# A third place for raw weight slabs: the tile of the probabilities, lent to the down projections and to one slab of the third block

## The chip, the cores and the metric

The kernel is one program on one core of a Trainium2 chip. The metric is the device time of a run in microseconds (us). The core's engines are TensorE (PE, matrix products; PEld is its weight load), VectorE (DVE), ScalarE (ACT), GpSimd (POOL) and SyncE (SP), which here only issues transfers. They run side by side and are held together by semaphores.

## The reference: three transformer blocks

The input x is 256 tokens by 1024. Two blocks of one kind run first, then one of another kind; all weights are float32 and each is used once.

```python
for l in range(2):                                   # first block, twice
    a = hybrid_mixer(rms_norm(x, pre_mix_g[l]), ...)
    x = x + rms_norm(a, post_mix_g[l])
    c = memory_cross_attention(rms_norm(x, pre_xattn_g[l]), rms_norm(mem, mem_g[l]), ...)
    x = x + rms_norm(c, post_xattn_g[l])
    hdn = jnp.square(jax.nn.relu(rms_norm(x, pre_mlp_g[l]) @ w_up[l]))
    x = x + rms_norm(hdn @ w_down[l], post_mlp_g[l])
h = rms_norm_2(x, norm_mix_g)                        # third block, once
z = h @ w_in                                         # gate, queries, keys/values, compress_blocks(...)
...
x = x + jnp.square(jax.nn.relu(h @ w_ff1)) @ w_ff2
```

The third block's attention first compresses keys and values with a small gelu network (`cmp_w1`, `cmp_w2`), whose weights are slabs 5 to 8 and 10 of that block.

## The kernel before: one stream of slabs through two raw places

Every weight matrix is cut into slabs of 128 partitions by 2048 float32 (1 MB). Blocks 0 and 1 have 64 slabs each, the third block has 59. A slab takes four steps, each by another engine:

1. SP issues its transfer from HBM into a raw place (`load`, L805; in the third block L837 and L839). There are two places, `raw[:, s % 2]`, so slab s waits until slab s-2 has been read for the last time (semaphore `slab_lo`).
2. ACT rounds it into `w_hi` (`split_hi`, L548). `w_hi` and `w_lo` are rings of three places, so this waits also until TensorE has finished slab s-3 (`slab_used`).
3. DVE subtracts the rounded part from the raw one and writes the rest into `w_lo` (`split_lo`, L558). That frees the raw place.
4. TensorE multiplies with `w_hi` and `w_lo`: 48 matmuls of 256 columns for a slab (for the down projections L2570, L2572, L2574).

Each engine works through a written order, with no scheduler behind it. SP issues slab after slab, in the order of the numbers, and one that waits holds back all behind it. ACT and DVE have `split_hi` and `split_lo` written between their other work, TensorE follows the tables `TE_ORDER` and `TE_ORDER_2`.

In blocks 0 and 1 the up projection is slabs 32 to 47 and the down projection slabs 48 to 63. In the third block they are slabs 27 to 42 and 43 to 58. During the up projection DVE writes each result, scaled and cut at zero, into one of the four places of the tile `probs` (L1656), and ACT squares it from there (`squared_up`, L1005 and L1006; the second counts the semaphore `h_sq`). In blocks 0 and 1 the last of these 16 squarings stands behind the rounding of slab 50 and ahead of that of slab 51. In the third block it stands behind the rounding of slab 45.

After the down projection come the sum of squares over the columns (DVE L1632, L1635; TensorE L2376), the root, the addition to x, and the first slabs of the next block. DVE has `split_lo` of the next block's slabs 0 and 1 ahead of L1632. Besides SP, POOL issues some transfers. During block 1's down projection it loads three tensors for the third block (L890 twice, L892), 1 MB in all as written.

In the third block ACT takes the root of a head's sum of squares in `head_root` (L1212). The third of these stands between the rounding of slab 7 and that of slab 8, with a load of the table for Exp behind it (`load_table`, L959). `head_inverse` on DVE (L1939, L1940) follows the root, and `split_lo` of slab 8 stands behind it. TensorE has the products of slab 7, then a turn (L2694), `head_spread` (L2687), and slab 8.

Of the kernel before, what the change touches and what calls it, by code (L numbers as in the profile page):

```python
# [139 lines left out]

FIRST_VALUES = 4

FIRST_CONSTANTS = 2
# [203 lines left out]
def build(nc, A, out):  # L347
    ctx = ExitStack()
    with ctx:
# [56 lines left out]
        sig = {name: sem(name) for name in PER}  # L406
        raw_loaded = [sem(f"raw_loaded{r}") for r in range(RAW)]
        i_load = {n: sem("i_" + n) for n in ("cst", "x", "mem", "gains", "pos", "relb", "rows", "skew", "toep", "gains_2",
# [126 lines left out]
        def slot(layer, s):  # L535
            return (64 * layer + s) % RING

        def split_hi(act, layer, s):


            loads = s // RAW + 1 + (second(layer) and s >= 3)
            act.wait_ge(raw_loaded[s % RAW], layer * (16 * 32) + 16 * loads)
            if 64 * layer + s >= RING:
                act.wait_ge(sig["slab_used"], value("slab_used", layer, s - RING + 1))
            pieces = split_views_2 if second(layer) else split_views
            views = pieces(s if s < 64 else 0, w_hi[:, slot(layer, s)], raw[:, s % RAW])
            for n, (d, r) in enumerate(views):
                ins = act.activation(d, r, ACT.Copy)  # L548
            ins.then_inc(sig["slab_hi"], 1)

        def split_lo(dve, layer, s):
# [3 lines left out]
            pieces = split_views_2 if second(layer) else split_views  # L555
            for (d, r), (h, _) in zip(pieces(sp, w_lo[:, slot(layer, s)], raw[:, s % RAW]),
                                      pieces(sp, w_hi[:, slot(layer, s)], raw[:, s % RAW])):
                ins = dve.tensor_tensor(d, r, h.bitcast(F32), ALU.subtract)  # L558
# [228 lines left out]
        def _(sp):  # L787
            for name in CREDIT:
# [7 lines left out]
                         A["x"][0].rearrange("(i p) n -> p i n", p=P)).then_inc(i_load["x"], 16)  # L796

            def load(layer, s):

                if (layer, s) in ((0, 0), (0, 1)):  # L800
                    return
                sp.wait_ge(sig["slab_lo"], value("slab_lo", layer, s - RAW + 1))
                src = slab_source(layer, s)
                a, b = src.shape[1], src.shape[2]
                sp.dma_start(raw[:, s % RAW, 0:a * b].rearrange("p (k n) -> p k n", k=a), src)\  # L805
                    .then_inc(raw_loaded[s % RAW], 16)

# [20 lines left out]

            for s in range(59):
                sp.wait_ge(sig["slab_lo"], v2("slab_lo", s - RAW + 1))  # L830
                src = slab_source_2(s)
                n = int(np.prod(src.shape[1:]))
                dst = raw[:, s % RAW, 0:n]
                if s in (3, 4):
                    dst = dst.rearrange("p (k v n) -> p k v n", k=8, v=2)
                    for v in range(2):
                        sp.dma_start(dst[:, :, v], src[:, :, v]).then_inc(raw_loaded[s % RAW], 16)  # L837
                else:
                    sp.dma_start(dst.rearrange("p (k n) -> p k n", k=src.shape[1]), src)\  # L839
                        .then_inc(raw_loaded[s % RAW], 16)  # L840
            for b in range(4):
# [74 lines left out]
        def _(act):  # L916
# [361 lines left out]
            for n in range(2):  # L1278
                act.wait_ge(once["sgw_turned"], n + 1)
                act.activation(sg_w[:, 4 * n:4 * n + 4], bank(f"sgw{n}", DEPTH)[:, :].rearrange(  # L1280
                    "p (g t) -> p g t", g=4), ACT.Copy).then_inc(once["sgw_evac"], 1)
            head_root(2, 8, 1.0, eps_64)
            load_table(ACT.Exp)
            split_hi(act, DEPTH, 8)
            split_hi(act, DEPTH, 9)
# [1653 lines left out]
```

## Time and profile before

| | |
|---|---|
| median of 3 runs | 1248.75 us (1247.89 to 1250.09) |
| the profiled execution | 1255.14 us, of which its span is 1253.3 us |
| PE busy | 1219.3 us, 97% of the span |
| PEld busy | 1188.8 us, 95% |
| DVE busy | 830.8 us, 66% |
| ACT busy | 666.8 us, 53% |
| POOL busy | 47.8 us, 4% |
| read from HBM | 198.50 MB, 159 GB/s over the span |

Busy time of PE is modelled and overlaps from one matmul to the next, so 97% doesn't mean that nothing is left. What is read here are the places where PE waits, and for whom. Times in rows are from the start of the span; the 1.8 us around it belong to the execution as well.

### The profile page before, as it was taken

Reading aid. Unit: us, or ns where it says so; the run is one execution under the profiler, and the core shown is the slowest. Engines: PE = TensorE matmul, PEld = TensorE weight load, DVE = VectorE, ACT = ScalarE, POOL = GpSimd, SP = SyncE. Lnnn points to the kernel's source line nnn. Section 1 sums busy time; section 2 is a strip of 40 time slices with the busy share of each in tenths; the row PEclk is TensorE's granted clock in tenths of the full one; section 3 lists DMA queues with packets and bytes.
Section 4 is the critical chain, followed back from the end, with each engine's and each line's share of the span. In section 5 each row is a group of like instructions: output and inputs, shape, how many; then the busy total and the mean of one; then the engine's idle time right before and its main releaser. Section 6 shows DMA issues by size and latency. Waiting matters only on the chain.

```text
span 1253.3 us, 23254 instructions
## 1 busy us (share of the span) xinstructions
PE 1219.3 (97%) x10089; PEld 1188.8 (95%) x10089; DVE 830.8 (66%) x972; ACT 666.8 (53%) x969; POOL 47.8 (4%) x45
## 2 busy tenths in 40 slices
PE   7999999999999999999999999989999999999998
PEld 6999999999999999999999999989899998999998
DVE  5797467677654678845868666348778875676442
ACT  5586455456544438645645654335486754555432
POOL 2100000000000000000000000100200100000000
PEclk9999999999999999999999999999989999999999
DMA  7735454346656453545434665663451543466552
GB/s 236 211 121 168 136 169 135 122 148 202 203 189 211 126 169 106 167 147 172 154 102 138 215 196 191 210 195 118 142 168 35 166 139 101 135 203 202 198 180 94
DMA packets 194840, 201.06 MB, mean 160 GB/s; under 512 B 5407, under 2 KB 191554, under 8 KB 194739
## 3 DMA queue, kind: packets, MB, share of 16 engines
q1 hardware_dynamic: 193155, 195.50, 48.6%
q0 software_dynamic: 1584, 4.08, 1.3%
q8 instruction: 80, 1.31, 0.5%
q14 instruction: 21, 0.17, 0.0%
HBM read 198.50 MB, written 1.26 MB: 159 GB/s over the span
## 4 chain that ended last, share of the span: by engine, by line
PE 77%; DVE 9%; DMA 5%; ACT 5%; issue 3%; SPq 0%; DVEq 0%; ACTq 0%
PE bank L602 13%; PE bank L603 13%; PE bank L604 13%; PE bank L2572 4%; PE bank L2570 4%; PE bank L2574 4%; DVE w_lo L558 4%; DMA raw<-in_w_down_dram 3%; ACT w_hi L548 3%; PE bank L645 2%; PE bank L653 2%; PE bank L647 2%; PE bank L2480 2%; PE bank L2464 2%; PE bank L701 2%
## 5 line engine op out<-in xcount | busy, mean ns | idle before, releaser
L558 DVE TENSOR_TENSOR w_lo<-raw,w_hi 128x2048 fp32r<-128x2048 f32 (+6 forms) x208 | 419.9, 2029 | 258.7 <-ACT w_hi L548 257.9
L548 ACT ACTIVATE w_hi<-raw 128x2048 fp32r<-128x2048 f32 (+6 forms) x208 | 351.7, 1703 | 336.3 <-PE bank L2574 68.6
L602 PE MATMUL bank<-act_hi,w_hi 128*128 128x256 f32 (+1 forms) x1104 | 307.6, 279 | 1.3 <-DVE w_lo L558 1.3
L604 PE MATMUL bank<-act_hi,w_lo 128*128 128x256 f32 (+1 forms) x1104 | 305.6, 277 | 0.0
L603 PE MATMUL bank<-act_lo,w_hi 128*128 128x256 f32 (+1 forms) x1104 | 305.6, 277 | 0.0
L602 PEld LDWEIGHTS bank<-act_hi,w_hi 128*128 128x128 f32 (+1 forms) x1104 | 206.9, 187 | 3.7 <-issue 3.3
L604 PEld LDWEIGHTS bank<-act_hi,w_lo 128*128 128x128 f32 (+1 forms) x1104 | 206.9, 187 | 0.1
L603 PEld LDWEIGHTS bank<-act_lo,w_hi 128*128 128x128 f32 (+1 forms) x1104 | 206.6, 187 | 0.2
L2570 PE MATMUL bank<-h_hi,w_hi 128*128 128x256 f32 x736 | 203.3, 276 | 0.0
L2574 PE MATMUL bank<-h_hi,w_lo 128*128 128x256 f32 x736 | 203.2, 276 | 0.0
L2572 PE MATMUL bank<-h_lo,w_hi 128*128 128x256 f32 x736 | 203.1, 276 | 0.0
L2572 PEld LDWEIGHTS bank<-h_lo,w_hi 128*128 128x128 f32 x736 | 138.2, 188 | 0.0
L2570 PEld LDWEIGHTS bank<-h_hi,w_hi 128*128 128x128 f32 x736 | 138.1, 188 | 0.0
L2574 PEld LDWEIGHTS bank<-h_hi,w_lo 128*128 128x128 f32 x736 | 138.1, 188 | 0.0
L602 PE MATMUL bank<-w_hi,act_hi 128*128 128x256 f32 (+1 forms) x272 | 78.2, 287 | 0.0
L603 PE MATMUL bank<-w_lo,act_hi 128*128 128x256 f32 (+1 forms) x272 | 76.4, 281 | 0.0
L604 PE MATMUL bank<-w_hi,act_lo 128*128 128x256 f32 (+1 forms) x272 | 76.3, 280 | 0.0
L645 PE MATMUL bank<-act_hi,w_hi 128*128 128x256 f32 x248 | 62.1, 284 | 5.8 <-ACT act_hi L923 5.7
L602 PE MATMUL bank<-o_hi,w_hi 128*128 128x256 f32 (+1 forms) x228 | 64.0, 281 | 0.9 <-issue 0.6
L603 PE MATMUL bank<-o_lo,w_hi 128*128 128x256 f32 (+1 forms) x228 | 63.5, 278 | 0.0
L604 PE MATMUL bank<-o_hi,w_lo 128*128 128x256 f32 (+1 forms) x228 | 63.4, 278 | 0.0
L647 PE MATMUL bank<-act_hi,w_lo 128*128 128x256 f32 x248 | 61.1, 280 | 0.0
(418 smaller groups left out, 2178.3 us busy)
## 6 DMA issues: line engine op xcount, KB each, us to landing
raw<-in_w_up_dram SPq DMA_DIRECT2D x32, 1024.0 KB, 5.4
raw<-in_w_down_dram SPq DMA_DIRECT2D x32, 1024.0 KB, 5.3
raw<-in_w_ff_dram SPq DMA_DIRECT2D x32, 1024.0 KB, 5.3
raw<-in_w_in_dram SPq DMA_DIRECT2D x21, 1024.0 KB, 5.4
raw<-in_w_xk_dram SPq DMA_DIRECT2D x8, 1024.0 KB, 5.3
raw<-in_w_xv_dram SPq DMA_DIRECT2D x8, 1024.0 KB, 5.2
raw<-in_w_mix_out_dram SPq DMA_DIRECT2D x8, 1024.0 KB, 5.2
raw<-in_w_xq_dram SPq DMA_DIRECT2D x8, 1024.0 KB, 5.4
```

What stands on the lines that cost most here:

```text
L548: ins = act.activation(d, r, ACT.Copy)
L558: ins = dve.tensor_tensor(d, r, h.bitcast(F32), ALU.subtract)
L602: pe.matmul(o, stat_hi, mov_hi, start=first, stop=False)
L603: pe.matmul(o, stat_hi, mov_lo, start=False, stop=False)
L604: return pe.matmul(o, stat_lo, mov_hi, start=False, stop=last)
L645: pe.matmul(dst, stat_hi, mov_hi, start=k == 0 and opens, stop=False, skip_group_check=True)
L647: pe.matmul(dst, stat_lo, mov_hi, start=False, stop=False, skip_group_check=True)
L653: ins = pe.matmul(dst, stat_hi, mov_lo, start=False, stop=k == 7, skip_group_check=True)
L701: pe.matmul(dst, wh[:, k, c], src_hi[:, k], start=opens and k == 4 * half and m == 0, stop=False, skip_group_check=True)
L2570: ins = pe.matmul(b[:, T * m:T * m + T], wh[:, k, cs], h_hi[:, 8 * c + k], start=c == 0 and k == 0 and (apart or m == 0), stop=False, skip ...
L2572: pe.matmul(b[:, T * m:T * m + T], wh[:, k, cs], h_lo[:, 8 * c + k], start=False, stop=False, skip_group_check=True)
L2574: ins = pe.matmul(b[:, T * m:T * m + T], wl[:, k, cs], h_hi[:, 8 * c + k], start=False, stop=c == 3 and k == 7, skip_group_check=True)
```

## The change: a table of places, a third place, and one slab ahead of its turn

A table `PLACES` now says of each slab which raw place it uses, how far that place's semaphore then stands, and which slab was there before. In the first 51 slabs of blocks 0 and 1, and the first 46 of the third block, the places are as before but for slab 8 of the third. From slab 51 (46) on they go round three: `probs`, `raw` 0, `raw` 1. The first slab of each block's round of three waits also for the last squaring (`h_sq` 16). In the third block slab 8 uses `probs` too: SP issues it between slabs 1 and 2, and ACT rounds it ahead of the third `head_root` instead of behind that and the table load. DVE's and TensorE's orders are the same.

```diff
+SPARE_FROM = {block: 51 for block in range(DEPTH)} | {DEPTH: 46}
+EARLY_SLAB = 8
+def slab_places():
+    table, last, loaded = {}, {}, {}
+    for block in range(DEPTH + 1):
+        for s in range(64 if block < DEPTH else 59):
+            first = SPARE_FROM[block]
+            if (block, s) == (DEPTH, EARLY_SLAB) or s >= first and (s - first) % 3 == 0:
+                place = RAW
+            else:
+                place = s % RAW if s < first else (s - first) % 3 - 1
+            loaded[place] = loaded.get(place, 0) + (32 if block == DEPTH and s in (3, 4) else 16)
+            table[block, s] = place, loaded[place], last.get(place)
+            last[place] = block, s
+    return table
...
-        raw_loaded = [sem(f"raw_loaded{r}") for r in range(RAW)]
+        raw_loaded = [sem(f"raw_loaded{r}") for r in range(RAW + 1)]
...
+        def raw_of(layer, s):
+            place = place_of(layer, s)[0]
+            if place == RAW:
+                return probs[:, :, :].rearrange("p u n -> p (u n)")
+            return raw[:, place]
...
+            def free_place(layer, s):
+                place, _, last = PLACES[layer, s]
+                if last is not None:
+                    sp.wait_ge(sig["slab_lo"], value("slab_lo", last[0], last[1] + 1))
+                if s == SPARE_FROM[layer]:
+                    sp.wait_ge(sig["h_sq"], value("h_sq", layer, 16))
+                return place
...
-                sp.wait_ge(sig["slab_lo"], value("slab_lo", layer, s - RAW + 1))
+                place = free_place(layer, s)
...
-            for s in range(59):
+            for s in (0, 1, EARLY_SLAB, *range(2, EARLY_SLAB), *range(EARLY_SLAB + 1, 59)):
...
+            split_hi(act, DEPTH, 8)
             head_root(2, 8, 1.0, eps_64)
             load_table(ACT.Exp)
-            split_hi(act, DEPTH, 8)
```

SP's instructions over block 0's down projection. Before (the row of `w_up` is the up projection, the last two rows are the next block's slabs 0 to 3):

```order
L805 DMA raw<-in_w_xo_dram 128x8x256 [waits slab_lo] x4
L805 DMA raw<-in_w_up_dram 128x8x256 [waits slab_lo] x16
L805 DMA raw<-in_w_down_dram 128x8x256 [waits slab_lo] x16
L805 DMA raw<-in_w_in_dram 128x8x256 [waits slab_lo] x3
L805 DMA raw<-in_w_in_dram 128x8x160 [waits slab_lo]
```

And now:

```order
L847 DMA raw<-in_w_up_dram 128x8x256 [waits slab_lo] x16
L847 DMA raw<-in_w_down_dram 128x8x256 [waits slab_lo] x3
L847 DMA probs<-in_w_down_dram 128x8x256 [waits h_sq]
L847 DMA raw<-in_w_down_dram 128x8x256 [waits slab_lo] x2
L847 DMA probs<-in_w_down_dram 128x8x256 [waits slab_lo]
L847 DMA raw<-in_w_down_dram 128x8x256 [waits slab_lo] x2
...
L847 DMA raw<-in_w_in_dram 128x8x256 [waits slab_lo] x3
```

The fourth transfer (slab 51) now waits for the last squaring instead of slab 49, and slabs 52 and 53 stand behind it in the same queue.

ACT's instructions at the third block's slab 8. The first row in each is slab 7, the row with 128x192 is slab 9; L1207 and L1249 are squares for the heads, L1280 and L1322 copy turned weights out of two banks. Before:

```order
L548 ACTIVATE w_hi<-raw 128x2048 [waits slab_used,raw_loaded1]
L1207 ACTIVATE head_sq<-q_t 128x512 [waits b2_hs_spread,b2_y_evac]
L1280 ACTIVATE toep<-bank1 128x512 [waits b2_sgw_turned]
L1280 ACTIVATE toep<-bank2 128x512 [waits b2_sgw_turned]
L1212 ACTIVATE small<-bank4,cst 128x8 [waits b2_hs_mm]
L959 ACT_TABLE_LOAD
L959 ACTIVATE small<-cst 128x1
L548 ACTIVATE w_hi<-raw 128x2048 [waits slab_used,raw_loaded0]
L548 ACTIVATE w_hi<-raw 128x192 [waits slab_used,raw_loaded1]
```

And now:

```order
L581 ACTIVATE w_hi<-raw 128x2048 [waits slab_used,raw_loaded1]
L1249 ACTIVATE head_sq<-q_t 128x512 [waits b2_hs_spread,b2_y_evac]
L1322 ACTIVATE toep<-bank1 128x512 [waits b2_sgw_turned]
L1322 ACTIVATE toep<-bank2 128x512 [waits b2_sgw_turned]
L581 ACTIVATE w_hi<-probs 128x2048 [waits slab_used,raw_loaded2]
L1254 ACTIVATE small<-bank4,cst 128x8 [waits b2_hs_mm]
L1001 ACT_TABLE_LOAD
L1001 ACTIVATE small<-cst 128x1
L581 ACTIVATE w_hi<-raw 128x192 [waits slab_used,raw_loaded1]
```

The rounding of slab 8 moved over three instructions and reads `probs` instead of `raw` 0.

## Rows read from the trace of the kernel before

**Rows 1.** The page's first part: engine, busy us, share, instructions.

```profile
PE 1219.3 (97%) x10089; PEld 1188.8 (95%) x10089; DVE 830.8 (66%) x972; ACT 666.8 (53%) x969; POOL 47.8 (4%) x45
```

**Rows 2.** Waits of PE over the span: us in total, times, longest.

```profile
PE bank L2376 <- DVE sumsq L1635: 4.9, 2, 4.7
PE bank L602 <- DVE w_lo L558: 3.5, 6, 2.1
```

**Rows 3.** The chain of waits, block 1's end: start us, us, what.

```profile
793.54 7.15 DMA raw<-in_w_down_dram
...
804.99 11.58 DMA raw<-in_w_down_dram
...
820.87 5.33 DMA raw<-in_w_down_dram
...
830.49 6.40 DMA raw<-in_w_in_dram
...
836.92 1.92 ACT w_hi L548
...
842.09 1.19 PE bank L2376 x2
```

**Rows 4.** DVE in order of time, same place: start, us, instruction, idle before.

```profile
838.86 2.29 DVE L558 TENSOR_TENSOR w_lo<-raw,w_hi 128x2048 fp32r<-128x2048 f32 x1 [5.51 <-ACT w_hi L548]
```

**Rows 5.** Waits from 733 to 842 (block 1): us in total, times, longest.

```profile
ACT w_hi L548 <- DMA raw<-in_w_down_dram: 40.5, 11, 8.7
```

**Rows 6.** Busy time by stretch: us, engines' busy us, PEclk, DMA share, GB/s.

```profile
425.90:430.70 4.80, 3.45 (x15) 2.60 (x16) 1.88 (x5) 1.64 (x4) 0.00 (x0) 1.00 0.48 137
842.10:848.40 6.30, 5.83 (x16) 4.60 (x16) 2.07 (x5) 1.64 (x4) 0.71 (x1) 0.51 1.04 300
893.10:896.10 3.00, 3.00 (x28) 2.56 (x27) 2.40 (x7) 2.66 (x4) 0.00 (x0) 1.00 0.66 173
899.50:904.00 4.50, 4.50 (x25) 3.50 (x25) 2.07 (x8) 1.23 (x4) 0.00 (x0) 0.62 0.25 47
```

**Rows 7.** DMA issues from 802 to 842: KB each, median us to landing.

```profile
toep<-in_sg_w_dram POOLq DMA_DIRECT2D x1, 512.0 KB, 10.6
```

**Rows 8.** ACT in order of time, block 0's last squaring and slab 52.

```profile
345.14 0.61 ACT L1006 ACTIVATE h_hi<-probs 128x512 fp32r<-128x512 f32 x1
...
350.00 1.92 ACT L548 ACTIVATE w_hi<-raw 128x2048 fp32r<-128x2048 f32 x1 [2.44 <-PE bank L2574]
```

**Rows 9.** The same in block 1.

```profile
756.81 0.61 ACT L1006 ACTIVATE h_hi<-probs 128x512 fp32r<-128x512 f32 x1
...
761.67 1.92 ACT L548 ACTIVATE w_hi<-raw 128x2048 fp32r<-128x2048 f32 x1 [2.43 <-PE bank L2574]
```

**Rows 10.** ACT, third block: the last squaring, then slabs 47 and 48.

```profile
1163.07 0.62 ACT L1006 ACTIVATE h_hi<-probs 128x512 fp32r<-128x512 f32 x1
...
1171.61 1.92 ACT L548 ACTIVATE w_hi<-raw 128x2048 fp32r<-128x2048 f32 x1 [3.52 <-PE bank L2574]
1177.05 1.92 ACT L548 ACTIVATE w_hi<-raw 128x2048 fp32r<-128x2048 f32 x1 [3.52 <-PE bank L2574]
```

**Rows 11.** DMA from 764 to 775: GB/s in 40 equal slices.

```profile
GB/s 0 0 0 0 0 0 123 67 194 346 350 372 380 391 384 391 384 380 354 346 350 324 343 343 343 331 335 350 231 37 22 26 22 26 22 26 82 11 0 0
```

**Rows 12.** The chain of waits, third block, ahead of slabs 6 and 8.

```profile
876.25 7.18 DMA raw<-in_cmp_w_dram
...
889.47 5.71 DMA raw<-in_cmp_w_dram
```

**Rows 13.** ACT in order of time ahead of slab 8.

```profile
890.61 1.07 ACT L1280 ACTIVATE toep<-bank 128x512 f32<-128x512 f32 x2
893.29 0.27 ACT L1212 ACTIVATE small<-bank,cst 128x8 f32<-128x8 f32 x1 [1.62 <-PE bank L2663]
```

**Rows 14.** DVE in order of time ahead of slab 8, and its `split_lo`.

```profile
895.14 0.43 DVE L1940 COPY head_sq<-small 128x512 f32<-128x512 f32 x1
897.14 2.29 DVE L558 TENSOR_TENSOR w_lo<-raw,w_hi 128x2048 fp32r<-128x2048 f32 x1 [1.57 <-ACT w_hi L548]
```

More of the change, by code:

```diff
@@ L141 @@
 FIRST_VALUES = 4
+SPARE_FROM = {block: 51 for block in range(DEPTH)} | {DEPTH: 46}
[13 more added lines that the diff above has]
+    return table
+PLACES = slab_places()
 FIRST_CONSTANTS = 2
@@ L536, in slot, with place_of @@
             return (64 * layer + s) % RING
+        def place_of(layer, s):
+            return PLACES[layer + s // 64, s % 64]
+        def raw_of(layer, s):
[3 more added lines that the diff above has]
+            return raw[:, place]
         def split_hi(act, layer, s):
-            loads = s // RAW + 1 + (second(layer) and s >= 3)
-            act.wait_ge(raw_loaded[s % RAW], layer * (16 * 32) + 16 * loads)
+            place, loaded, _ = place_of(layer, s)
+            act.wait_ge(raw_loaded[place], loaded)
             if 64 * layer + s >= RING:
@@ L545, in split_hi @@
             pieces = split_views_2 if second(layer) else split_views
-            views = pieces(s if s < 64 else 0, w_hi[:, slot(layer, s)], raw[:, s % RAW])
+            views = pieces(s if s < 64 else 0, w_hi[:, slot(layer, s)], raw_of(layer, s))
             for n, (d, r) in enumerate(views):
@@ L555, in split_lo @@
             pieces = split_views_2 if second(layer) else split_views
-            for (d, r), (h, _) in zip(pieces(sp, w_lo[:, slot(layer, s)], raw[:, s % RAW]),
-                                      pieces(sp, w_hi[:, slot(layer, s)], raw[:, s % RAW])):
+            for (d, r), (h, _) in zip(pieces(sp, w_lo[:, slot(layer, s)], raw_of(layer, s)),
+                                      pieces(sp, w_hi[:, slot(layer, s)], raw_of(layer, s))):
                 ins = dve.tensor_tensor(d, r, h.bitcast(F32), ALU.subtract)
@@ L801, in load @@
                     return
-                sp.wait_ge(sig["slab_lo"], value("slab_lo", layer, s - RAW + 1))
+                place = free_place(layer, s)
                 src = slab_source(layer, s)
                 a, b = src.shape[1], src.shape[2]
-                sp.dma_start(raw[:, s % RAW, 0:a * b].rearrange("p (k n) -> p k n", k=a), src)\
-                    .then_inc(raw_loaded[s % RAW], 16)
+                sp.dma_start(raw_of(layer, s)[:, 0:a * b].rearrange("p (k n) -> p k n", k=a), src)\
+                    .then_inc(raw_loaded[place], 16)
             for half in range(2):
@@ L827, in _ @@
                     load(layer, s)
-            for s in range(59):
-                sp.wait_ge(sig["slab_lo"], v2("slab_lo", s - RAW + 1))
+            for s in (0, 1, EARLY_SLAB, *range(2, EARLY_SLAB), *range(EARLY_SLAB + 1, 59)):
+                place = free_place(DEPTH, s)
                 src = slab_source_2(s)
                 n = int(np.prod(src.shape[1:]))
-                dst = raw[:, s % RAW, 0:n]
+                dst = raw_of(DEPTH, s)[:, 0:n]
                 if s in (3, 4):
@@ L836, in _ @@
                     for v in range(2):
-                        sp.dma_start(dst[:, :, v], src[:, :, v]).then_inc(raw_loaded[s % RAW], 16)
+                        sp.dma_start(dst[:, :, v], src[:, :, v]).then_inc(raw_loaded[place], 16)
                 else:
                     sp.dma_start(dst.rearrange("p (k n) -> p k n", k=src.shape[1]), src)\
-                        .then_inc(raw_loaded[s % RAW], 16)
+                        .then_inc(raw_loaded[place], 16)
             for b in range(4):
```

## The prediction, written before the changed kernel ran

> **What bounds the kernel now.** The page comes first: PE is busy 1219.3 of 1253.3 us [rows 1], so raw places can only pay where PE waits for a slab, or for work that stands behind a slab. The waits of PE come second. For a slab it waits 3.5 us in all, 2.1 of them at one place. For `sumsq`, the sum of squares after a down projection, it waits twice, 4.7 us and 0.2 us [rows 2]. Third is the chain of waits at the longer one. There the products of block 1's last slab are done, and TensorE's next step comes only at 842.09. Ahead of it the chain runs transfer, rounding, remainder, transfer, with single transfers of 7.15, 11.58, 5.33 and 6.40 us [rows 3]. The last of them is slab 1 of the third block: it lands at 836.89, is rounded until 838.84, and DVE makes its remainder from 838.86 to 841.15 [rows 3, 4]. The two additions of `sumsq` stand behind that on DVE. So a late raw slab holds TensorE up, though it is not the slab's own products that are late. In block 1's stretch ACT waited 11 times for a transfer, 40.5 us in all [rows 5]; with two places a transfer can't start before the slab two earlier has gone through ACT and DVE.
>
> The other blocks don't have this. In the third block's down projection ACT waits 3.52 us for TensorE before each slab, which is the ring of three rounded slabs being full [rows 10]. A third raw place gives nothing there. In block 0 the same step as at 842.09 waited 0.2 us [rows 2].
>
> **The steps that I use.** A slab takes TensorE 1177.05 - 1171.61 = 5.44 us [rows 10], ACT 1.92 us [rows 3] and DVE 2.29 us [rows 4]. A transfer on its own lands 5.3 us after issue [rows 3]. Two slabs behind one another moved at about 350 GB/s [rows 11], 1.05 MB in 3.0 us, so of several in flight each lands 3.0 us after the one ahead, if they go one after the other.
>
> **Part 1, the wait for the last squaring (blocks 0 and 1).** Slab 51 used to be issued at once when slab 49 was read; now it waits for `h_sq` 16, and slabs 52 and 53 stand behind it on SP. In block 0 that squaring ends at 345.75 [rows 8]. Issue 345.8, landing 351.1, rounding to 353.0, remainder to 355.3. TensorE ended slab 49 at 350.0 [rows 8], so it asks for slab 51 at 355.4. In block 1: squaring done 757.42, landing 762.8, remainder ready 767.05; TensorE ended slab 49 at 761.67 [rows 9] and asks at 767.1. Both arrive with 0.1 us to spare, and a transfer that is 0.5 us slower than 5.3 costs that much. I take 0.2 us for each block, bounds 0 and 0.5. Slabs 52 and 53 land 3 and 6 us behind 51, at 765.8 and 768.8 in block 1; their remainders, at 770 and 773, are asked for at 772.5 and 778.0. No cost. In the third block the last squaring ends at 1163.69, and slab 46 would be ready at 1163.7 + 5.3 + 1.92 + 2.29 = 1173.2; it is asked for at 1177.05, when slab 45 ends [rows 10]. No cost.
>
> **Part 2, the end of block 1.** From slab 55 on the ring of rounded slabs is full, as it is in the third block, and rounding follows TensorE: slab s starts when slab s-3 ends, that is at 767.1 + 5.44 (s - 53) or so. Slab 58 is rounded at 794.3 and read by 798.5, so slab 61 is issued at 798.5 instead of 804.99 and is in before POOL's three loads move. One transfer will still meet these loads (sg_w itself took 10.6 us [rows 7]): slab 62, issued when slab 59 is read, at 804.0. With 11.6 us, as slab 61 had, it lands at 815.6, and ACT asks for it when slab 59 ends, at 767.1 + 9 x 5.44 = 816.1. The cushion covers it with 0.5 us left, and TensorE needs the result only 10.9 - 4.2 = 6.7 us later than ACT asks. Slabs 63, 0 and 1 are then never late, and the wait shrinks to block 0's 0.2 us: -4.5 us [rows 2].
>
> The Trainium skill ("DMA: Bandwidth & Descriptors", section "Queues, rings and completion order") says that a DMA engine goes round the queue rows that have work, a packet of each at a time. By that rule a third slab in SP's queue wins no bandwidth from POOL's loads, and the 11.6 us stay. The trace has one such meeting only and can't tell a fair share from a block. The sum above gives the third slab no share either, so it stands under both.
>
> **The clock there.** After the long wait PE was granted 0.51 of its clock for 842.1 to 848.4, that is the lower level, 1.2 GHz; the same steps took 4.8 us at full clock in block 0 and 6.3 us here [rows 6]. Without the wait I expect the full clock: -1.5 us.
>
> **Part 3, slab 8 of the third block.** TensorE waits 2.1 us for its remainder [rows 2]. It was issued at 889.47 when slab 6 was read [rows 12]. Now it has been in `probs` for 50 us, and ACT rounds it right behind the copies at 891.67, until 893.6 [rows 13]. The root that stood at 893.29 slips to 893.6, so DVE's last copy for that head ends at 895.9 instead of 895.57, and the remainder, which DVE has behind it, runs from 895.9 to 898.2 instead of 897.14 to 899.43 [rows 14]. That is -1.2 us, not -2.1: the wait on ACT is replaced by DVE's order. TensorE's spread of that root begins at 896.2 and still finds it. Between 899.5 and 904.0 the clock was granted at 0.62, and 24 products took 4.5 us instead of 3.0 [rows 6]; about 0.9 us of wait is left, so I leave that cost where it is and keep -1.5 us as the bound.
>
> **The sum, and what a run without the profiler has.** Against the profiled execution's own 1255.14 us: +0.4 -4.5 -1.5 -1.2 = -6.8, 1248.3 us. But that execution is 6.4 us over the median of 1248.75, more than the spread of the three runs, and the wait at 842 is just what a few slow transfers make. If the 7.15 and the 6.40 us in [rows 3] were 5.3, the wait would be some 3 us shorter, 1.7, and only 1.5 us of it could go. Slab 6's 7.18 us in front of slab 8 [rows 12] is such a case too: at 5.3, slab 8 would have come some 1.2 us earlier before as well, and part 3 would give nothing. POOL's loads come in every run. I take the middle: end of block 1 -3.0, clock -1.5, part 3 -0.6, part 1 +0.4: -4.7, near 1244.1 us. Bounds: -4.5 -1.5 -1.2 -1.5 = -8.7 (1240.0) and -1.5 + 1.0 = -0.5 with no clock to win (1248.2).
>
> **Rivals.**
> - *The wait belongs to the profiled run alone.* For it: the 6.4 us above the median are nearly its 4.7 + 1.5. Against: the longest transfer in the chain is the one beside POOL's loads, and they are in the program. What is left is part 3 against part 1, -0.6 + 0.4: 1248.5 us.
> - *The cushion is used up.* If slabs 51 to 54 start late enough that the ring is not full by slab 58, slab 62 is late too and the wait at 842 is only halved. For it: 0.5 us of margin. Against: each slab gains 5.44 - 3.0 us while transfers are in a row. -1.5 - 0.6 + 0.4, 1247.0 us.
> - *Three transfers in flight share instead of queue (slower).* Slabs 51, 52 and 53 are now issued within 1 us. If their packets mix, 51 lands with the last, 5.3 + 6.0 = 11.3 us after issue, and TensorE waits 5.9 us in block 0 and again in block 1, most likely with the lower clock behind it (+1.5 each, [rows 6]): +14.8, less the 4.7 + 0.4 that the rest brings, 1258.4 us. It decides from a landing 7.9 us after issue, where two waits of 2.5 us eat the gain. For it: all go through one queue to the same 16 engines. Against: rows 11 show 350 GB/s while two slabs were in flight, so nothing is lost by it, but not in which order they came.
> - *The place isn't worth its wait:* the change does what it says, but slab 51's delay is the size of the upper bound in both blocks and a little of the clock goes: +1.0 against -1.5: no change.
>
> The Trainium skill, same page and section, has each engine consume its descriptors in ring order, though a later one may finish its write first. By that slab 51 lands first and the third rival is out; its chance below is what these rows leave open.
>
> **How the numbers follow.** The main forecast 0.58, the first rival 0.18, the second 0.10, the third 0.07, the last 0.07. A measurement of this kernel tells about 0.2%, 2.5 us, from no change. Of the main forecast nearly all is faster by more than that (0.54 of 0.58), of the second rival a little (0.03); all of the first and last is within it, and the third is slower, with a little of the last: faster 0.57, same 0.34, slower 0.09. The main forecast's own range is 1241.5 to 1246.5; the range for 8 in 10 takes in the first two rivals and the lower bound, 1240.0 to 1249.0.
>
> **What would show it.** Right: the wait for `sumsq` L1635 near 0.2 us at both places; the granted clock at 1.0 there; ACT's waits for `w_down` fewer from slab 55 on, and waits of 3.5 us for PE in their place; slab 8's remainder right behind L1940 on DVE, 1.2 us earlier. Wrong: PE waiting for `w_lo` in L2570 near slab 51, a first transfer of three that lands over 6 us after issue, or a transfer over 12 us beside POOL's loads with the wait for `sumsq` still there.

## The result, and the profile after

| | median us | lowest to highest | runs |
|---|---|---|---|
| before | 1247.81 | 1243.06 to 1254.71 | 20 |
| after | 1252.76 | 1244.93 to 1255.01 | 20 |

The ratio is 1.0033, 95% interval 1.0020 to 1.0045: the changed kernel is slower by some 4 us (2.5 to 5.6), and the prediction of 1244.1 us, with 57% on faster, was wrong. The profiled execution of after took 1253.64 us (span 1251.8), that of before 1255.14 (span 1253.3). So the two traces alone would say "1.5 us faster". Both kernels' executions differ among themselves by over 10 us, and most of this section is about why.

Three views of after answer to [rows 1, 2]: the page's first part, the waits of PE (engine, line, what it waited for: us in total, times, longest), and two groups of instructions (busy us, mean ns of one). L2612 and L2616 of after are L2570 and L2574 of before, L635 is L602, L591 is L558, L581 is L548, L2418 is L2376.

```profile
PE 1222.2 (98%) x10089; PEld 1192.3 (95%) x10089; DVE 831.1 (66%) x972; ACT 666.7 (53%) x969; POOL 47.6 (4%) x45
```

```profile
PE bank L635 <- DVE w_lo L591: 2.5, 6, 0.7
...
PE bank L2612 <- DVE w_lo L591: 0.8, 2, 0.5
```

```profile
L2612 PE MATMUL bank<-h_hi,w_hi 128*128 128x256 f32 x736 | 205.4, 279 | 0.8 <-DVE w_lo L591 0.8
L2616 PE MATMUL bank<-h_hi,w_lo 128*128 128x256 f32 x736 | 205.1, 279 | 0.0
```

The wait for `sumsq` of 4.9 us is gone, and the longest wait for `w_lo` has shrunk from 2.1 to 0.7. In their place there are two short waits in the down projections, 0.8 us together. Yet PE is busy 2.9 us *longer* with the same 10089 instructions: the matmuls of the down projections average 279 ns and not 276. The same two groups on the page of before:

```profile
L2570 PE MATMUL bank<-h_hi,w_hi 128*128 128x256 f32 x736 | 203.3, 276 | 0.0
L2574 PE MATMUL bank<-h_hi,w_lo 128*128 128x256 f32 x736 | 203.2, 276 | 0.0
```

Three nanoseconds of 279 look like nothing. They are an average over blocks that don't agree, as PE in order of time shows at slab 51 of block 0 (start us, us, instruction, idle before):

```profile
355.30 0.28 PE L2614 MATMUL bank<-h_lo,w_hi 128*128 128x256 f32 x1
355.41 0.28 PE L2616 MATMUL bank<-h_hi,w_lo 128*128 128x256 f32 x1
355.94 0.36 PE L2612 MATMUL bank<-h_hi,w_hi 128*128 128x256 f32 x1 [0.26 <-DVE w_lo L591]
356.13 0.28 PE L2614 MATMUL bank<-h_lo,w_hi 128*128 128x256 f32 x1
356.25 0.28 PE L2616 MATMUL bank<-h_hi,w_lo 128*128 128x256 f32 x1
356.37 0.28 PE L2612 MATMUL bank<-h_hi,w_hi 128*128 128x256 f32 x1
```

The start-to-start time is 0.53 us at the stall, where it would have been 0.11. Before it the starts are 113 ns apart (355.30, 355.41), behind it 118 (356.13, 356.25, 356.37), and so it stays for the rest of the block. Busy time by stretch (us, busy us with instructions of PE, PEld, DVE, ACT, POOL, then PEclk, DMA share, GB/s), after, ahead of the stall and behind it, in block 0 and in block 1:

```profile
267.60:354.20 86.60, 86.60 (x765) 86.57 (x764) 60.34 (x54) 47.91 (x49) 0.00 (x0) 1.00 0.62 198
356.20:415.00 58.80, 58.80 (x501) 58.80 (x501) 26.16 (x13) 24.63 (x18) 2.91 (x1) 1.00 0.63 209
683.30:770.00 86.70, 86.70 (x765) 86.65 (x764) 60.07 (x54) 47.72 (x49) 0.00 (x0) 1.00 0.62 197
772.60:830.00 57.40, 57.40 (x489) 57.40 (x489) 25.91 (x12) 24.07 (x18) 4.91 (x4) 1.00 0.73 225
```

86.60 / 765 = 113.2 ns a matmul ahead, 58.80 / 501 = 117.4 behind (117.8 where single starts are compared). PE is busy all the time and its granted clock is 1.00 in all four rows, so neither the busy share nor the clock shows that anything is wrong; only the count does. A slab of 48 matmuls takes 5.65 us instead of the 5.44 of [rows 10], which the grid of ACT's rounding shows too, since it follows TensorE there:

```profile
373.24 1.92 ACT L581 ACTIVATE w_hi<-raw 128x2048 fp32r<-128x2048 f32 x1 [3.74 <-PE bank L2616]
378.89 1.92 ACT L581 ACTIVATE w_hi<-probs 128x2048 fp32r<-128x2048 f32 x1 [3.74 <-PE bank L2616]
```

From slab 51 on that is some 13 slabs x 0.21 = 2.7 us for each block. Another matter, at slab 8 of the third block, went better than I had it; it comes with experiment 2.

**One ruler for all runs.** Ahead of slab 35 of blocks 0 and 1, and of slab 29 of the third, TensorE runs six matmuls with both operands from `w_hi` (`weights_first`). I take their first start, and the first start of the sums behind the last slab (`ones` by `v_dil`), as marks. For block 0 of after they are these two rows, the stretch 430.80 - 267.57 = 163.23 us:

```profile
267.57 0.70 PE L2412 MATMUL bank<-w_hi 128*128 128x256 f32 x3
```

```profile
430.80 0.48 PE L2447 MATMUL bank<-v_dil,ones 128*128 128x256 f32 x1 [0.47 <-ACT v_dil L1016]
```

Worked out in this way from the starts in each trace (the start-to-start time at slab 51 in brackets where there is a stall, then S where the stream stays at 117.8 ns behind it, F where it is back at 113.3 within a few matmuls):

| kernel | block 0 | block 1 | third, up to slab 29 |
|---|---|---|---|
| before | 160.18 | 165.51 | 239.0 |
| before, second profile | 160.18 | 160.33 | 237.9 |
| after | 163.23 (0.53, S) | 163.50 (0.80, S) | 235.1 |
| after, second profile | 161.05 (0.88, F) | 160.87 (0.71, F) | 234.0 |
| after, third profile | 163.42 (0.71, S) | 160.75 (0.58, F) | 236.1 |
| 1: from slab 52 | 160.18 | 160.18 | 235.0 |
| 1, second profile | 160.18 | 160.18 | 232.7 |
| 2: slab 8 alone | 160.18 | 160.35 | 232.8 |
| 3: after, `w_hi` matmuls at 52 | 161.31 (0.43, F) | 162.67 (1.59, S, then F) | 234.1 |
| 4: before, slab 51 late | 163.21 (0.51, S) | 163.69 (0.84, S) | 238.6 |
| 4, second profile | 160.72 (0.57, F) | 163.58 (0.88, S) | 236.2 |
| 5: before, pause at 47 of the third | 160.18 | 161.30 | 236.4 |
| 6: downs alone, from 52 | 160.18 | 160.18 | 236.0 |
| 7: after, plain matmuls at 52 | 163.63 (0.67, S, then F) | 164.58 (1.61, S, then F) | 235.0 |

### The profile page after: what moved, and what is told of

Read it like the earlier page. It is cut to its first block, busy times and chain, and to the rows that moved or that the text cites. A ratio compares the mean times of both kernels' runs of the same rounds, so it can differ in the third digit from the quotient of the medians.

```text
span 1251.8 us, 23256 instructions
## 1 busy us (share of the span) xinstructions
PE 1222.2 (98%) x10089; PEld 1192.3 (95%) x10089; DVE 831.1 (66%) x972; ACT 666.7 (53%) x969; POOL 47.6 (4%) x45
## 4 chain that ended last, share of the span: by engine, by line
PE 81%; DVE 8%; ACT 5%; issue 3%; DMA 3%; SPq 0%; DVEq 0%; ACTq 0%
PE bank L635 13%; PE bank L636 13%; PE bank L637 13%; PE bank L2612 6%; PE bank L2614 6%; PE bank L2616 6%; DVE w_lo L591 3%; ACT w_hi L581 2%; PE bank L678 2%; PE bank L686 2%; PE bank L680 2%; PE bank L2522 2%; PE bank L734 2%; PE bank L736 1%; PE bank L735 1%
## 5 line engine op out<-in xcount | busy, mean ns | idle before, releaser
L591 DVE TENSOR_TENSOR w_lo<-raw,w_hi 128x2048 fp32r<-128x2048 f32 (+5 forms) x192 | 383.4, 2007 | 212.2 <-ACT w_hi L581 211.9
L581 ACT ACTIVATE w_hi<-raw 128x2048 fp32r<-128x2048 f32 (+5 forms) x192 | 321.0, 1684 | 280.0 <-PE bank L2616 72.3
L635 PE MATMUL bank<-act_hi,w_hi 128*128 128x256 f32 (+1 forms) x1104 | 308.3, 279 | 2.1 <-DVE w_lo L591 2.1
L635 PEld LDWEIGHTS bank<-act_hi,w_hi 128*128 128x128 f32 (+1 forms) x1104 | 207.3, 188 | 4.5 <-issue 4.1
L2612 PE MATMUL bank<-h_hi,w_hi 128*128 128x256 f32 x736 | 205.4, 279 | 0.8 <-DVE w_lo L591 0.8
L2616 PE MATMUL bank<-h_hi,w_lo 128*128 128x256 f32 x736 | 205.1, 279 | 0.0
L2612 PEld LDWEIGHTS bank<-h_hi,w_hi 128*128 128x128 f32 x736 | 139.0, 189 | 1.1 <-issue 1.1
L2616 PEld LDWEIGHTS bank<-h_hi,w_lo 128*128 128x128 f32 x736 | 138.2, 188 | 0.0
L635 PE MATMUL bank<-w_hi,act_hi 128*128 128x256 f32 (+1 forms) x272 | 78.3, 288 | 0.3 <-DVE probs L1566 0.3
L591 DVE TENSOR_TENSOR w_lo<-probs,w_hi 128x2048 fp32r<-128x2048 f32 x16 | 36.7, 2292 | 45.3 <-ACT w_hi L581 45.3
L635 PE MATMUL bank<-o_hi,w_hi 128*128 128x256 f32 (+1 forms) x228 | 64.1, 281 | 0.9 <-issue 0.6
```

The lines of the kernel that those rows point to most:

```text
L635: pe.matmul(o, stat_hi, mov_hi, start=first, stop=False)
L2612: ins = pe.matmul(b[:, T * m:T * m + T], wh[:, k, cs], h_hi[:, 8 * c + k], start=c == 0 and k == 0 and (apart or m == 0), stop=False, skip ...
L2616: ins = pe.matmul(b[:, T * m:T * m + T], wl[:, k, cs], h_hi[:, 8 * c + k], start=False, stop=c == 3 and k == 7, skip_group_check=True)
```

## The experiments

The theory after the comparison: slab 51's late issue stalls TensorE in each block, and the stall leaves the stream of 256-column matmuls at the slower of two spacings. In the recorded expectations this is theory A. The rivals (theory B): the third slab in flight slows the transfers, or writing raw slabs into `probs` costs something itself.

**1. The third place one slab later.** The wait for the last squaring moves to slab 52, everything else stays.

```
-SPARE_FROM = {block: 51 for block in range(DEPTH)} | {DEPTH: 46}
+SPARE_FROM = {block: 52 for block in range(DEPTH)} | {DEPTH: 46}
```

> The round of three places starts with slab 52 instead of 51 in blocks 0 and 1; slab 51 is issued when slab 49 is read, as in the kernel before. Theory A (cadence): TensorE's 256-column matmuls start either 113.3 or 117.8 ns apart, and a short wait of TensorE inside the stream (0.4 and 0.7 us at slab 51 in the changed kernel) leaves it at the slower one, 5.65 us a slab instead of 5.44, until something else resets it. Without the wait: slabs 51 to 63 of both blocks at 5.44 us, the waits at slab 51 gone, the wait for sumsq near 0.2 us, so 6 to 7 us under the changed kernel, median near 1245. Theory B (traffic): three transfers in flight, or the slabs written to and read from the tile of the probabilities, slow TensorE's operand reads. Then the slabs stay at 5.65 us with three places in use, and only the waits of 1.1 us go: near 1251.

Measured: 1243.77 us (1240.52 to 1247.24, 12 runs) against 1246.86 (32 runs), ratio 0.9977 (0.9964 to 0.9990). It is 2.9 us under the kernel before (1.2 to 4.5), and so under the changed kernel too. The third place is used from slab 52 on, `probs` is written, three slabs are in flight, and there is no stall. Busy time by stretch, around the same place:

```profile
300.00:350.00 50.00, 50.00 (x444) 50.00 (x443) 35.44 (x34) 26.64 (x27) 0.00 (x0) 1.00 0.61 193
356.00:406.00 50.00, 50.00 (x443) 50.00 (x443) 21.32 (x10) 20.34 (x15) 2.92 (x1) 1.00 0.59 198
```

444 and 443 matmuls in 50 us: the spacing doesn't change. Both rivals fall, since all that they blame is in this kernel. Theory A had put it near 1245. A second profile gave the same 160.18 us in both blocks and 1244.69 us:

> The changed kernel with the third place from slab 52 in blocks 0 and 1, a second profile. No stall at slab 51 or 52, both blocks again 160.18 us from slab 35 to the end at 113.3 ns; third block to slab 29 about 235 us against 236.0 to 239.0 in the runs with slab 8 in its old order.

**2. Slab 8 alone.** The third place serves slab 8 of the third block only.

```
-SPARE_FROM = {block: 51 for block in range(DEPTH)} | {DEPTH: 46}
+SPARE_FROM = {block: 64 for block in range(DEPTH + 1)}
```

> Only slab 8 of the third block uses the third place and is rounded early; all down projections use two places as before. Both theories: down projections at 5.44 us a slab as before, the wait for sumsq at block 1's end of 0 to 4.7 us as before, slab 8's remainder right behind DVE's copy for the head, 1.2 us earlier or less. Median 0 to 2 us under the kernel before.

Measured: 1244.78 us (1242.01 to 1248.26), ratio 0.9979 (0.9967 to 0.9991), 2.1 us under the 1246.86 of before, where 0 to 2 had been expected. So slab 8 carries more than my 0.6 us. What it carries is at one place. PE, second profile of before, and busy time of the 4 us from there:

```profile
893.83 0.30 PE L602 MATMUL bank<-w_hi,o_hi 128*30 128x256 f32 x1 [1.94 <-DVE w_lo L558]
```

```profile
893.80:897.80 4.00, 3.97 (x24) 3.24 (x24) 2.12 (x8) 1.23 (x4) 0.00 (x0) 0.66 0.18 39
```

The same two of after:

```profile
899.51 0.30 PE L635 MATMUL bank<-w_hi,o_hi 128*30 128x256 f32 x1 [0.38 <-DVE w_lo L591]
```

```profile
899.50:903.50 4.00, 3.99 (x38) 3.58 (x39) 2.50 (x9) 1.12 (x4) 0.00 (x0) 1.00 0.03 6
```

The wait goes from 1.94 to 0.38. It is 1.9 to 2.1 us in all six profiles with the old order and at most 0.4 in the eight with slab 8 early. Directly behind it the granted clock is 1.00 here and not 0.66: 38 matmuls in 4 us instead of 24. But that low clock is no fixed part of the wait. It stands behind it in four of the six old profiles (both of before, the first of experiment 4, experiment 6) and is missing in two. Experiment 5, which is the kernel before up to here:

```profile
892.03 0.30 PE L602 MATMUL bank<-w_hi,o_hi 128*30 128x256 f32 x1 [1.92 <-DVE w_lo L558]
```

```profile
892.00:896.00 4.00, 3.97 (x36) 3.56 (x37) 2.52 (x9) 1.23 (x4) 0.00 (x0) 1.00 0.18 39
```

A further stretch of 3.4 to 10.2 us at the lower clock begins between 904 and 917 us in all 14 profiles, with either order; it didn't go.

The table's last column has the sum: 236.0 to 239.0 us, mean 237.4, in the six profiles with the old order, 232.7 to 236.1, mean 234.4, in the eight with slab 8 early: 3.0 us. The four old ones with the low clock average 237.9, the two without 236.3. The medians put slab 8 at 2.1 us (1.1 to 4.1).

The other finding is in the waits from 830 to 840 us, where this kernel has two raw places as before had:

```profile
PE bank L2418 <- DVE sumsq L1677: 0.4, 1, 0.4
```

0.4 us, not 4.7. Together with the second profile of before (below) this says that the long wait of [rows 2] belongs to the one execution shown.

**3. Six matmuls from `w_hi` behind the stall.** The changed kernel with, ahead of slab 52, what it already does ahead of slab 35:

```
+                    if (kind, n) == ("slab", 52):
+                        weights_first(layer, 52, "down1", 6)
```

> The changed kernel, with six matmuls more ahead of slab 52 in blocks 0 and 1 that read both operands from the rounded slab, as the kernel already has ahead of slabs 19 and 35 (their results are overwritten). Theory A: if such a run of matmuls puts TensorE back at 113.3 ns, slabs 52 to 63 take 5.44 us again: 12 x 0.21 = 2.5 us back for each block, less 0.7 us for the six: 3 to 4 us under the changed kernel. If it stays at 117.8 ns: 1.4 us over it. Theory B: 1.4 us over it.

Measured: 1248.79 us (1247.17 to 1251.16), ratio 1.0016 (1.0002 to 1.0029). Busy time ahead of them and behind them, block 1:

```profile
768.40:773.80 5.40, 5.40 (x48) 5.40 (x47) 4.59 (x2) 2.08 (x2) 0.00 (x0) 1.00 0.87 296
774.90:780.30 5.40, 5.40 (x50) 5.40 (x49) 2.29 (x1) 2.12 (x4) 0.00 (x0) 1.00 0.82 256
```

The slow stretch lasted one slab, from 768.1 to 773.8 us, and then the stream was at 113.3 ns up to the block's end. The stalls are still there (0.43 and 1.59 us), so this kernel pays for them and for 12 added matmuls and is 1.9 us slower than before (0.2 to 3.6), but not as the changed kernel is. That is some 2 us under the changed kernel where I had expected 3 to 4. In block 1 slab 51's transfer took 6.3 us here and in experiment 7, where 5.3 to 5.5 had been seen, which accounts for most of the longer stall. In block 0 the stream was fast again before the added matmuls, so block 1 is the one case that tests them. In all 14 profiles of this study together there are 72 groups of these matmuls (with four or six of them); the stream is at 113.3 ns behind all 72, and was at 117.8 ahead of 57. Yet 70 of them stand right behind matmuls of still other forms, so they are weaker evidence for this form than the one case.

**4. The late slab without the third place.** The kernel before, with two raw places, and slab 51 issued behind the last squaring:

```
+                if s == 51:
+                    sp.wait_ge(sig["h_sq"], value("h_sq", layer, 16))
```

> The kernel before with two raw places, but slab 51's transfer waits for the last squaring as in the changed kernel; no third place anywhere. Theory A: TensorE waits 0.3 to 0.8 us at slab 51 in blocks 0 and 1, and slabs 51 to 63 then take 5.65 us: 5 to 7 us over the kernel before. Theory B: slabs stay at 5.44 us, at most 1.5 us over the kernel before.

Measured: 1253.12 us (1249.91 to 1259.06, 9 runs), ratio 1.0052 (1.0033 to 1.0070). PE at slab 51 of block 0, and busy time ahead of and behind it:

```profile
353.62 0.28 PE L2576 MATMUL bank<-h_hi,w_lo 128*128 128x256 f32 x1
354.13 0.36 PE L2572 MATMUL bank<-h_hi,w_hi 128*128 128x256 f32 x1 [0.23 <-DVE w_lo L558]
```

```profile
300.00:350.00 50.00, 50.00 (x444) 50.00 (x443) 36.18 (x34) 25.84 (x28) 0.00 (x0) 1.00 0.55 177
356.00:406.00 50.00, 50.00 (x427) 50.00 (x426) 22.13 (x11) 19.90 (x15) 2.92 (x1) 1.00 0.63 211
```

A stall of 0.4 us, and 427 matmuls in 50 us where there had been 444. One wait on SP is enough for the damage: +6.3 us (4.1 to 8.7) where theory A had 5 to 7, with nothing of the third place in the kernel. Its second profile:

> The kernel before with slab 51 issued after the last squaring, again: two more stalls without the third place. Same two values as for the changed kernel: 163.2 to 163.7 us where the stall leaves the stream slow, 160.9 to 161.1 where not. If the slow spacing were bound to the third place (rival), this kernel would show it less often than the changed one; its first profile had it in both blocks.

It took 1251.87 us: block 0 kept 113.3 ns through its stall, block 1 did not. So the slow spacing is not certain.

**5. A pause of another kind.** The kernel before; in the third block TensorE waits ahead of slab 47 until slab 49 has been rounded.

```
+                    if s == 47:
+                        pe.wait_ge(sig["slab_hi"], v2("slab_hi", s + 3))
```

> The kernel before with one edit: in the third block's down projections TensorE waits, ahead of slab 47, until ScalarE has rounded slab 49. Nothing is moved in any queue, no third place. The pause is about 2.0 us by the traces (slab 49's high half ends about 2 us after slab 47 could have begun). Theory A (a short pause in the stream of 256-column matmuls leaves it at the slower spacing, 117.8 ns instead of 113.3): the third block's last 12 slabs take 5.65 us each instead of 5.44, 12 x 0.21 = 2.5 us on top of 2.0, so about 4.5 us slower than before (ratio 1.0036). Rival B (a pause costs its own length and no more): 2.0 us (ratio 1.0016), and the spacing after it stays at 113.3 ns. Where the stream has turned slow by itself before slab 47, A also gives only 2.0.

Measured: 1252.03 us (1248.77 to 1256.0, 8 runs), ratio 1.0032 (1.0016 to 1.0048), +4.0 us. But its profile is the fastest of the eight, and in it the pause (2.38 us from start to start) was not followed by the slow spacing; ACT's grid behind it is still 5.44:

```profile
1181.56 1.92 ACT L548 ACTIVATE w_hi<-raw 128x2048 fp32r<-128x2048 f32 x1 [5.89 <-PE bank L2574]
1187.00 1.92 ACT L548 ACTIVATE w_hi<-raw 128x2048 fp32r<-128x2048 f32 x1 [3.52 <-PE bank L2574]
```

Theory A in the form "a short pause leaves the stream slow" had to be given up for "a stall may leave it slow". The median is where A put it (4.5) rather than the rival (2.0), but the interval, 2.0 to 6.0, holds both, and the trace that exists is of the other kind. Inconclusive for the price, clear against certainty.

**6. The downs alone, from slab 52.** As experiment 1, with slab 8 back in its old order.

```
+SPARE_FROM = {block: 52 for block in range(DEPTH)} | {DEPTH: 46}
+EARLY_SLAB = None
```

> The third place in the down projections alone, from slab 52 in blocks 0 and 1 and from slab 46 in the third block; slab 8 of the third block stays in its old order. The kernel with slab 8 early and the third place from 52 was 2.9 us under before, the one with slab 8 early alone 2.1 us. If slab 8 carries the gain: within 1 us of before (1246 to 1247.5). If the downs carry one of their own (the wait for the sum of squares gone at the end of block 1): 1.5 to 3 us under before. Slabs at 113.3 ns spacing in blocks 0 and 1 up to the last, as in the kernel before.

Measured: 1248.07 us (1244.61 to 1249.66, 12 runs) against 1248.03, ratio 0.9998 (0.9984 to 1.0012). The third place in the down projections, without a stall, is worth nothing that can be measured. So experiment 1's gain is slab 8's, as far as this interval (-2.0 to +1.5 us) tells.

**The two kernels once more**, for a second profile of each:

> The kernel before, for a second profile. The wait of 4.7 us at the end of block 1 for the sum of squares: if it belongs to the kernel, it is there again at 3 us or more; if it belonged to the profiled execution shown, it is under 1 us, as in the runs with slab 8 alone early.

1249.27 us. Its waits from 835 to 842 us:

```profile
PE bank L2376 <- DVE sumsq L1635: 0.3, 1, 0.3
```

> The changed kernel, for a second profile. Theory A: the gaps of 0.5 to 0.8 us ahead of slab 51 in blocks 0 and 1 come again, with the spacing at 117.8 ns behind them to the end of each block. If one of the two blocks has no gap, its spacing stays at 113.3 ns and the span is some 3 us shorter.

1246.45 us, with stalls of 0.88 and 0.71 us from start to start and the fast spacing behind both. PE at the first of them:

```profile
354.24 0.28 PE L2616 MATMUL bank<-h_hi,w_lo 128*128 128x256 f32 x1
355.12 0.36 PE L2612 MATMUL bank<-h_hi,w_hi 128*128 128x256 f32 x1 [0.61 <-DVE w_lo L591]
```

A longer stall than that at 355.41 in the first profile, and no slow stretch, where I had expected one: the length doesn't decide. The third profile:

> The changed kernel, a third profile: two more stalls at slab 51. Each of 0.4 to 1.6 us. If a stall draws the spacing anew: each block at 117.8 ns or at 113.3 up to its end, never between, the stretch from slab 35 to the end 163.2 to 163.5 or 160.9 to 161.1 us (160.18 in both blocks without a stall). Third block from its start to slab 29: 234 to 235 us, as in all five runs with slab 8 early.

1250.74 us, block 0 slow, block 1 fast. The three profiles of one kernel, with two, one and no slow blocks, took 1253.64, 1250.74 and 1246.45 us. The 20 timed runs fall into groups at the same heights, which fits, though it doesn't show, that they have two, one and no slow blocks: 11 from 1252.4 up, 4 from 1250.3 to 1251, 5 from 1244.9 to 1248.7.

**7. Plain matmuls in the same place.** Is it the operands of experiment 3 that restore the spacing, or any matmuls of another form?

```
+                    if (kind, n) == ("slab", 52):
+                        keep_clock(layer, "down1", 6)
```

> The changed kernel with six plain matmuls (identity by a constant tile, 256 columns) ahead of slab 52 of blocks 0 and 1, in the place where the earlier run had six matmuls with both operands from w_hi. The stall at slab 51 (0.5 to 1.6 us) comes in both blocks in either. Theory A' (a stall draws the spacing of the stream anew, 113.3 or 117.8 ns, and only matmuls with both operands from w_hi set it to 113.3): the plain ones do not restore it, some blocks stay at 117.8 ns up to their end, stretch from slab 35 to the end of a block 163.9 to 164.2 us where it is slow (163.2 to 163.5 plus six matmuls of 0.11), median as of the changed kernel plus 1.4 us, 4 to 5 over before. Rival (any matmuls of another form restore it): both blocks at 113.3 ns behind slab 52, 161.7 us a block, median as with the w_hi matmuls, about 2 over before. By the rival of chance alone (a block may fall fast anyway) one block fast proves nothing, both slow proves the rival wrong.

Measured: 1252.43 us (1248.25 to 1258.2, 12 runs), ratio 1.0036 (1.0019 to 1.0054). PE ahead of, at and behind them, block 0:

```profile
361.15 0.28 PE L2614 MATMUL bank<-h_lo,w_hi 128*128 128x256 f32 x1
361.27 0.28 PE L2616 MATMUL bank<-h_hi,w_lo 128*128 128x256 f32 x1
361.39 2.75 PE L2404 MATMUL bank<-cst 128*128 128x256 f32 x12
363.79 0.47 PE L2612 MATMUL bank<-h_hi,w_hi 128*128 128x256 f32 x1
...
364.34 0.28 PE L2612 MATMUL bank<-h_hi,w_hi 128*128 128x256 f32 x1
364.45 0.28 PE L2614 MATMUL bank<-h_lo,w_hi 128*128 128x256 f32 x1
```

118 ns ahead, 113 behind, in this block and in block 1. My theory (only the `w_hi` operands do it) fell: the rival was right for both blocks. The median still came out where the fallen theory had it, for a reason that neither had counted: six plain matmuls, whose operands are not rounded as `w_hi` is, are 12 instructions of 215 ns, 2.6 us a block and not 0.7. A median that fits is no proof where the trace is at hand.

But "any matmuls of another form" is too wide as well. In the third block's down projection four matmuls of `cst` by `x_t` stand in the stream, at two places of each profile. The second profile of after, at the first of them and for 20 us on either side:

```profile
1193.66 0.60 PE L2869 MATMUL bank<-cst,x_t 128*128 128x128 f32 x4
```

```profile
1173.60:1193.60 20.00, 20.00 (x179) 20.00 (x178) 9.77 (x5) 6.25 (x4) 0.00 (x0) 1.00 0.58 192
1194.60:1214.60 20.00, 20.00 (x173) 20.00 (x172) 8.82 (x5) 7.46 (x5) 0.00 (x0) 1.00 0.62 203
```

From 179 matmuls to 173, with no wait there: a fast stream was slow behind these four. Of the 28 such places in the 14 profiles 20 were fast ahead and behind, 6 fast ahead and slow behind, 2 slow on both sides.

Over all profiles a stall at slab 51 (14 blocks) or at 47 (one) left the stream slow 9 times of 15, with stalls of 0.51 to 1.61 us from start to start, and fast 6 times, with 0.43 to 2.38. The first starts behind the stalls say more than that. In all 15 the first spacing is 192 to 195 ns and the next 116 to 120: each stall does put the stream at the slow spacing. In the six it is back at 113 to 115 ns two to five spacings behind the stall; in the nine it isn't. What brings it back is open.

## Why the prediction was wrong

**Part 1 failed; it is the step that turned the sign.** It priced the late slab 51 at 0.2 us a block. Its arithmetic of the transfer was nearly right. In block 0 of after the squaring ends at 346.09, slab 51 is issued at 346.12, and ACT and DVE have it as follows:

```profile
351.47 1.93 ACT L581 ACTIVATE w_hi<-probs 128x2048 fp32r<-128x2048 f32 x1 [5.38 <-DMA probs<-in_w_down_dram]
```

```profile
353.50 2.29 DVE L591 TENSOR_TENSOR w_lo<-probs,w_hi 128x2048 fp32r<-128x2048 f32 x1 [2.48 <-ACT w_hi L581]
```

The remainder is there 9.7 us behind the squaring, where I had 9.55, and TensorE starts 0.15 us after that. But it would have begun 9.43 behind the squaring, and I had 9.65: I took ACT's start at 350.00 [rows 8] for the end of slab 49 on TensorE. The last matmul of slab 49 and the first of slab 50, before:

```profile
349.63 0.28 PE L2574 MATMUL bank<-h_hi,w_lo 128*128 128x256 f32 x1
349.74 0.28 PE L2570 MATMUL bank<-h_hi,w_hi 128*128 128x256 f32 x1
```

Slab 51 is asked for at 349.74 + 5.44 = 355.18 and not at 355.4, so by the trace of before the cushion of 0.1 us was a lack of 0.1. The ten blocks of after and of experiment 4 show stalls of 0.4 to 0.8 us beyond the usual spacing, all above my middle and six of them past the upper end (0.5) of my bound. That alone is a mis-sized term: 1.1 to 1.4 us for both blocks instead of 0.4. What was missing as a mechanism is what a stall does to the stream behind it: 2.7 us more in 6 of these 10 blocks. I priced a wait at its own length. [Rows 10] gave 5.44 us a slab and I took that for a constant; a second spacing stood in the page of before, whose groups of 256-column matmuls average 276 ns in the down projections and 281 in the group `w_lo` by `act_hi`, and I didn't ask why.

**Part 2: mechanism right, size from one odd execution.** The wait for `sumsq` is gone, the clock there is full (1.00 from 844 to 852 us), the ring of rounded slabs is full: ACT's waits from 772 to 846 us are for TensorE now, where [rows 5] has 40.5 us for transfers,

```profile
ACT w_hi L581 <- PE bank L2616: 36.2, 11, 3.7
...
ACT w_hi L581 <- DMA raw<-in_w_down_dram: 3.0, 2, 2.1
```

and with slab 51 on time the stretch is exactly 160.18 us in all four blocks of experiment 1. But before had only 0.15 and 1.1 us to lose there in its two usual profiles (160.33 and 161.30; the latter is experiment 5, unchanged up to there). I had taken -3.0 and -1.5. The first rival ("the wait belongs to the profiled run alone") was right in this, and I gave it 0.18 after having written down its best argument: the profiled execution was 6.4 us above the median.

**Part 3: mechanism right, size too small.** Taken -0.6, measured about -3.0 in the traces and -2.1 in the medians of experiment 2. I held that a fast slab 6 would leave nothing to gain; the wait for slab 8 was 1.9 to 2.1 us in all six profiles of the old order. And I left the lower clock behind the wait where it was, since 0.9 us of wait should remain; 0.4 or less remained, and the clock right behind it stayed at 1.00 in all eight. That is -1.6 for the wait and about -1.5 for the clock in executions that had the low clock there, four profiles of six.

**The sum with measured terms.** Stalls +1.2, slab 8 -3.0, end of block 1 -0.2 to -1.1 and 2.7 for each slow block: about -2.4 with none slow, +0.3 with one, +3.0 with two. The measured +4 (2.5 to 5.6) lies at the two-slow end, though 6 of 10 blocks in the profiles are slow, which would give +0.8. Either the executions without a profiler are slow more often, or some 3 us (1.7 at the lower end of the interval) have a cause that I have not found; the runs don't tell. With slab 8 at the -2.1 of experiment 2 the gap is 1 us less. The slow spacing isn't confined to these stretches either: outside them 2300 to 3260 starts of each profile are 116 to 120 ns behind the one before, and at 4.5 ns each that alone moves executions by up to 4 us. These counts are close in before (2624 and 2857) and in after (2853 to 2953).

**The other rivals.** *Three transfers share instead of queue*: wrong. Slab 51 landed 5.3 us (block 0) and 5.5 us (block 1) after issue in the first profile of after, the two behind it 8.4 and 9.8 us after theirs in block 0. The DMA issues from 344 to 352 us (KB each, median us from issue to landing):

```profile
raw<-in_w_down_dram SPq DMA_DIRECT2D x2, 1024.0 KB, 9.1
probs<-in_w_down_dram SPq DMA_DIRECT2D x1, 1024.0 KB, 5.3
```

The Trainium skill ("DMA: Bandwidth & Descriptors", section "Queues, rings and completion order") has an engine take the descriptors of one ring in order; the trace agrees, 5.3 us as for a transfer alone. *The cushion is used up*: the ring was full in time, and no wait was left at the end of block 1. *The place isn't worth its wait*: nearest to what happened, but I gave it 0.07 and priced each stall at its own length. Of what I named as signs of a wrong forecast, "PE waiting for `w_lo` near slab 51" is the one that came.

## What to carry to other kernels

Price a wait inside a dense stream of matmuls by what follows it as well as by its length: compare the spacing of starts (count in a stretch by its time) ahead of it and behind it, not the busy share. Before a wait is moved onto a transfer whose result is used with a cushion of 0.1 us, move it one step later; here one slab turned +4 us into -3. Take the start of an engine's next step from that engine's own rows, not from the one that waits for it: here that was 0.26 us, more than the cushion. And take a term from the place where a profiled execution exceeds the median only after a second profile has shown it again.

## What the runs showed of the hardware that I had not expected

- TensorE runs the same stream (fp32 as rounded pairs, 256 columns, a new stationary operand for each matmul) at 113.3 or at 117.8 ns a matmul, with the granted clock at 1.00 in both. Behind each of 15 stalls the stream was at the slower one first; six times it was fast again after two to five spacings, nine times it stayed slow, up to the block's end or, three times, up to the matmuls that were added a slab later. The Trainium skill ("TensorE: Matmul & The Clock Gate", section "Back-to-back issue gap") gives the spacing of pairs of weight load and matmul as one number for each size that it lists; here there are two for one size. What decides whether it stays slow is open: neither the stall's length nor the third place does.
- Matmuls of another form in between can change it either way. It was at 113.3 ns behind all 72 groups with both operands from `w_hi` and behind both groups of unrounded ones at 215 ns an instruction, but at 117.8 behind 8 of 28 groups of `cst` by `x_t`. Why is open too.
- Behind a wait of 2 us at slab 8 the granted clock was 0.62 to 0.66 over the next 4 to 4.5 us in four profiles of six ([rows 6] and experiment 2), that is the lower level, 1.2 GHz, for most of it, and 1.00, 2.4 GHz, in the other two; behind a wait of 0.4 us or less at the same place it was 1.00 in all eight.
